# Fewer ready-made transposed tiles: 31 instead of 40, none of them made during the attention heads

## The reference, cut to what matters

```
h = rms(x) ; P = h @ w_in -> q,k,v (3 x 1024 columns) and B,C,xc (3 x 1024 columns)
attn = 8 heads of differential attention (two softmaxes a head, QK norm, ALiBi)
conv = B * causal_conv3(C * xc)
x = x + concat(attn, conv) @ w_out
h2 = rms(x)
PEER: q = h2 @ w_q ; top-16 of 128 keys twice per head -> 16 of 16384 experts, 8 heads
x = x + sum over chosen experts of  v[e] * gelu(u[e] . h2) * gate
```

## Time and profile before

| | us |
|---|---|
| runs of the kernel | 3073.46, 3074.99, 3070.95 (median 3073.46) |
| the profiled execution, its own time | 3075.95 |
| its span | 3074.1 |
| PE busy in the span | 2942.8 (96%) |
| DVE busy | 2327.9 (76%) |
| ACT busy | 1013.9 (33%) |
| POOL busy | 1505.5 (49%) |
| L1215, the 160 transposes of DVE | 100.2 |
| mean granted clock of TensorE | 0.987 of full |

### The profile page before, as it was taken

One profiled execution on the slowest core, in us unless ns is written; L12 is line 12 of the kernel. 1 busy time (PEld: TensorE's weight loads), 2 busy tenths in 40 slices (PEclk: granted clock), 3 DMA queues, 4 the chain that ended last, 5 costly groups with the idle time before them and its releaser, 6 DMA issues.

```text
span 3074.1 us, 40948 instructions
## 1 busy us (share of the span) xinstructions
PE 2942.8 (96%) x15249; PEld 2612.5 (85%) x15249; DVE 2327.9 (76%) x3102; ACT 1013.9 (33%) x1245; POOL 1505.5 (49%) x906
## 2 busy tenths in 40 slices
PE   8999989899988999999999999999999999998999
PEld 6888767678878999999999999999998877877777
DVE  5444656664468898888889887788766988988898
ACT  3112323341223333333333333233323333333333
POOL 1000222210006666555656665566766877886762
PEclk9999999999999999999999999999999999999999
DMA  7777676767458898989989898899999999999998
GB/s 262 261 235 222 204 212 186 219 237 273 150 183 290 293 339 301 319 297 326 317 296 342 298 320 299 297 334 318 322 354 368 413 414 410 415 415 415 416 415 338
DMA packets 321776, 947.12 MB, mean 308 GB/s; under 512 B 62484, under 2 KB 179232, under 8 KB 232288
## 3 DMA queue, kind: packets, MB, share of 16 engines
q1 hardware_dynamic: 177040, 475.04, 42.7%
q0 software_dynamic: 107008, 439.75, 40.5%
q10 hardware_dynamic: 37584, 30.43, 3.0%
HBM read 849.56 MB, written 95.55 MB: 307 GB/s over the span
## 4 chain that ended last, share of the span: by engine, by line
PE 63%; DVE 13%; DMA 12%; issue 6%; ACT 4%; POOL 0%; ACTq 0%; DVEq 0%; SPq 0%; POOLq 0%
PE ps L1695 19%; PE ps L1697 19%; PE ps L1696 19%; DMA v_raw<-in_peer_v 8%; PE ps L1945 4%; DMA seg_rows<-in_peer_u 3%; DVE v_lo L1608 2%; DVE u_row L1569 2%; ACT v_hi L1096 1%; DVE uT_lo L1553 1%; DVE seg_turned L1215 1%; DVE uT_lo L1558 1%; DVE wc_lo L1184 1%; ACT uT_hi L1056 1%; DVE x_one L1650 0%
## 5 line engine op out<-in xcount | busy, mean ns | idle before, releaser
L1695 PE MATMUL ps<-hT_hi,uT_hi 128*128 128x384 f32 x2048 | 703.2, 343 | 28.3 <-DVE uT_lo L1553 25.0
L1697 PE MATMUL ps<-h2T_lo,uT_hi 128*128 128x384 f32 x2048 | 688.2, 336 | 0.0
L1696 PE MATMUL ps<-hT_hi,uT_lo 128*128 128x384 f32 x2048 | 687.0, 335 | 0.0
L759 POOL DMA_INDIRECT gate_grid<-gates,grid_cells x256 | 542.2, 2118 | 120.2 <-issue 76.5
L1695 PE MATMUL ps<-v_hi,a_hi 128*128 128x512 f32 x1024 | 405.2, 396 | 35.0 <-DVE v_lo L1608 33.4
L1695 PEld LDWEIGHTS ps<-hT_hi,uT_hi 128*128 128x128 f32 x2048 | 386.3, 189 | 38.3 <-DVE uT_lo L1553 31.1
L1697 PE MATMUL ps<-v_lo,a_hi 128*128 128x512 f32 x1024 | 402.6, 393 | 0.0
L1696 PE MATMUL ps<-v_hi,a_lo 128*128 128x512 f32 x1024 | 402.6, 393 | 0.0
L1096 ACT ACTIVATE v_hi<-v_raw 128x2048 fp32r<-128x2048 f32 x128 | 245.7, 1919 | 462.2 <-PE ps L1697 345.4
L1696 PEld LDWEIGHTS ps<-hT_hi,uT_lo 128*128 128x128 f32 x2048 | 386.6, 189 | 1.9
L1697 PEld LDWEIGHTS ps<-h2T_lo,uT_hi 128*128 128x128 f32 x2048 | 385.8, 188 | 0.0
(11 more groups left out here) (206 smaller groups left out, 4860.1 us busy)
## 6 DMA issues: line engine op xcount, KB each, us to landing
v_raw<-in_peer_v SPq DMA_DIRECT2D x128, 1024.0 KB, 15.2
u_tile<-in_peer_u SPq DMA_DIRECT2D x88, 1024.0 KB, 7.2
seg_rows<-in_peer_u SPq DMA_DIRECT2D x40, 1024.0 KB, 6.7
u_tile<-uT_all SPq DMA_DIRECT2D x40, 1024.0 KB, 7.3
uT_all<-seg_turned SPq DMA_DIRECT2D x100, 256.0 KB, 6.4
w_raw<-in_w_in SPq DMA_DIRECT2D x24, 1024.0 KB, 6.3
wc_raw<-in_w_in SPq DMA_DIRECT2D x48, 512.0 KB, 7.4
gate_grid<-zeros POOLq DMA_DIRECT2D x16, 1024.0 KB
```

The costliest lines, as they stand in the source:

```text
L759: pool.indirect_dma_start(out=gate_grid, out_offset=bass.IndirectOffsetOnAxis(ap=grid_cells[:, d, col:col + 1], axis=0), in_=gates[:, 2 + ...
L1695: mm(out, a_hi, b_hi, start=first, stop=False)
L1696: mm(out, a_lo, b_hi, start=False, stop=False)
L1697: return mm(out, a_hi, b_lo, start=False, stop=last)
```

## The change

The heads make no ready-made tiles any more. Each of the five chunks in the loop of the projections makes four (the fourth after the split of the next chunk's quarter 1). The three at the end of the projections stay (now numbers 21, 22 and 23), and the seven in the output projection. All stores are issued by SP, none by POOL. The sweep finds 31 tiles ready (1, 3, ... 61) and lets PE transpose the other 97.

```diff
-TURNED = 40
-TURNED_QKV = 3 * (QKV_CHUNKS - 1)
-TURNED_HEADS = TURNED_QKV + 4 + 2 * (HEADS - 1)
-KEPT_BY_POOL = 1 + 2 * (HEADS - 1)
-KEPT_BY_SP = TURNED - KEPT_BY_POOL
+TURNED = 31
+TURNED_QKV = 4 * (QKV_CHUNKS - 1)
+TURNED_FIRST = TURNED_QKV + 4
...
 # SP, load_weights, behind load_quarter of every quarter
-                        if turned is not None and (q > 0 and turned == 0 if isinstance(c, int) else q != 1):
-                            keep_turned(3 * c + (turned + max(q - 1, 0)))
+                        if turned == 0 and not (isinstance(c, int) and q == 0):
+                            keep_turned(4 * c + (q - 1))
+                        elif turned is not None and turned > 0 and not isinstance(c, int) and q != 1:
+                            keep_turned(3 * c + (turned - 3 + max(q - 1, 0)))
...
 # SP, between the projections and the heads
             conv_piece(0, 0)
             conv_piece(0, 1)
-            for n in range(2):
-                keep_turned(TURNED_QKV + 1 + n)
+            for n in range(3):
+                keep_turned(TURNED_QKV + 1 + n, last=n == 2)
             with sp.Fori(0, CT - 1) as j:
                 for p in range(PIECES):
                     sp.wait_ge(wc_ready, PIECES * j + p + 1)
                     conv_piece(j + (p + 2) // PIECES, (p + 2) % PIECES)
-                    if p in (3, 5):
-                        next_rows(2 * j + (TURNED_QKV + 3 + p // 5))
...
 # POOL: the stores of number 18 and of two tiles a head are gone
-            keep_turned(TURNED_QKV + 3)
...
-                    keep_turned(TURNED_QKV + 4 + 2 * j)
...
-                    keep_turned(TURNED_QKV + 5 + 2 * j)
...
 # DVE, the loop of the projections
                 split_wi(c, 2)
-                turn_rows(3 * c + 1, "qkv")
+                turn_rows(4 * c + 1)
                 split_wi(c, 3)
-                turn_rows(3 * c + 2, "qkv")
+                turn_rows(4 * c + 2)
                 split_wi(c + 1, 0)
                 keep_qkv(c)
-                turn_rows(3 * c + 3, "qkv")
+                turn_rows(4 * c + 3)
                 split_wi(c + 1, 1)
+                turn_rows(4 * c + 4)
...
 # DVE, a head
                 combined(0)
-                if not last:
-                    turn_rows(2 * j + (TURNED_QKV + 4), "heads", range(2))
                 biased(2)
                 combined(1)
-                if not last:
-                    turn_rows(2 * j + (TURNED_QKV + 4), "heads", range(2, 4))
                 biased(3)
...
                 if not last:
-                    turn_rows(2 * j + (TURNED_QKV + 5), "heads")
                     norm_qk(j + 1, 1)
```

More of the change, by code:

```diff
@@ L408, in decoder_layer @@
         seg_stored = sem("seg_stored")
-        seg_kept = sem("seg_kept")
         u_tile_in = sems("u_tile_in", 2)
@@ L462, in load_rows @@
                 sp.dma_start(seg_rows[:, :], u_table[bass.ds((2 * n + 1) * P, P), :]).then_inc(seg_in, 16)
-            def next_rows(n):
-                sp.wait_ge(seg_ready, 4 * n + 4)
-                load_rows(n + 1)
             def keep_turned(n, last=False):
@@ L487, in load_weights @@
                     sp.wait_ge(w_used[0], QKV_CHUNKS + 1)
-                    load_rows(turned + 3)
+                    load_rows(turned)
                 with sp.Fori(1, chunks - 1) as c:
@@ L493, in load_weights @@
                     load_quarter(weights, chunks - 1, q + 2, order)
-                    if turned is not None and q == 0:
-                        keep_turned(turned + 3 * (chunks - 1), last=turned > 0)
+                    if turned == 0:
+                        keep_turned(4 * (chunks - 1) + q - 1)
+                    elif turned is not None and q == 0:
+                        keep_turned(3 * (chunks - 1) + turned - 3, last=True)
             for t in range(TB):
@@ L550, in _ @@
             load_mix(MIX_ORDER[3])
-            load_weights(OUT_CHUNKS, w_out_v, QKV_CHUNKS, MIX_ORDER, begun=3, turned=TURNED_HEADS - 3)
+            load_weights(OUT_CHUNKS, w_out_v, QKV_CHUNKS, MIX_ORDER, begun=3, turned=TURNED_FIRST)
             sp.wait_ge(w_ready, 4 * (QKV_CHUNKS + OUT_CHUNKS) - 1)
@@ L595, in _ @@
             sp.wait_ge(wq_ready, 4)
-            sp.wait_ge(seg_stored, 16 * QUADS * KEPT_BY_SP)
-            sp.wait_ge(seg_kept, 16 * QUADS * KEPT_BY_POOL)
+            sp.wait_ge(seg_stored, 16 * QUADS * TURNED)
             for i in range(PEER_HEADS - 2):
@@ L705, in zero_cells @@
                                zeros[:, :].unsqueeze(1).to_broadcast([P, 8, GRID])).then_inc(grid_done, 16)
-            def keep_turned(n):
-                pool.wait_ge(seg_ready, 4 * n + 4)
-                store_turned(pool, n, seg_kept)
-            keep_turned(TURNED_QKV + 3)
             pool.wait_ge(head_mean, 1)
@@ L718, in _ @@
                     store_o(j - 1)
-                if j < HEADS - 1:
-                    keep_turned(TURNED_QKV + 4 + 2 * j)
                 pool.wait_ge(head_mean, 2 * j + 2)
@@ L828, in split_weights @@
                 if isinstance(c, int) and (c, before) == (0, QKV_CHUNKS) and q < 2:
-                    act.wait_ge(seg_kept, 16 * QUADS * KEPT_BY_POOL)
+                    act.wait_ge(seg_stored, 16 * QUADS * TURNED_FIRST)
                     nc.scalar.activation((wo0_hi if q == 0 else w_hi[1])[:, :, :], wo_raw0, ACT.Copy).then_inc(w_hi_ready, 1)
@@ L996, in split_wq @@
                 nc.scalar.activation(part[:, :, :], raw[:, :, :], ACT.Copy).then_inc(wq_hi_ready, 1)
-            act.wait_ge(seg_stored, 16 * QUADS * KEPT_BY_SP)
+            act.wait_ge(seg_stored, 16 * QUADS * TURNED)
             split_wq(0, 0, early=True)
@@ L1201, in _, with turn_rows @@
             low(0, 3)
-            def turn_rows(n, stage, parts=range(4)):
-                if parts[0] == 0:
-                    dve.wait_ge(seg_in, 16 * n + 16)
-                    if isinstance(n, int) and n == 0:
-                        pass
-                    elif stage == "heads":
-                        dve.wait_ge(seg_kept, 16 * QUADS * (n - (TURNED_QKV + 3)))
-                    else:
-                        dve.wait_ge(seg_stored, 16 * QUADS * (n if stage == "qkv" else n - KEPT_BY_POOL))
-                for q in parts:
+            def turn_rows(n):
+                dve.wait_ge(seg_in, 16 * n + 16)
+                if not (isinstance(n, int) and n == 0):
+                    dve.wait_ge(seg_stored, 16 * QUADS * n)
+                for q in range(4):
                     v.transpose(seg_turned[:, :, 4 * q:4 * q + 4, :].rearrange("p r k e -> p k r e"),
@@ L1217, in turn_rows @@
                         .then_inc(seg_ready, 1)
-            turn_rows(0, "qkv")
+            turn_rows(0)
             dve.wait_ge(vec_in, 16 * 10)
@@ L1238, in _ @@
                 split_wi(c, 2)
-                turn_rows(3 * c + 1, "qkv")
+                turn_rows(4 * c + 1)
                 split_wi(c, 3)
-                turn_rows(3 * c + 2, "qkv")
+                turn_rows(4 * c + 2)
                 split_wi(c + 1, 0)
                 keep_qkv(c)
-                turn_rows(3 * c + 3, "qkv")
+                turn_rows(4 * c + 3)
                 split_wi(c + 1, 1)
+                turn_rows(4 * c + 4)
             split_wi(chunks - 1, 2)
-            turn_rows(TURNED_QKV + 1, "qkv")
+            turn_rows(TURNED_QKV + 1)
             split_wi(chunks - 1, 3)
-            turn_rows(TURNED_QKV + 2, "qkv")
+            turn_rows(TURNED_QKV + 2)
             dve.wait_ge(w_used[2], chunks)
@@ L1254, in _ @@
             keep_qkv(chunks - 1)
-            turn_rows(TURNED_QKV + 3, "qkv")
+            turn_rows(TURNED_QKV + 3)
             split_wc(0, 2)
@@ L1407, in rest_of_chunk @@
                 if not first:
-                    turn_rows(3 * c + (TURNED_HEADS - 1), "out")
+                    turn_rows(3 * c + (TURNED_FIRST - 1))
                 split_wo(c + 1, 0)
@@ L1411, in rest_of_chunk @@
                     add_mixed(c, t)
-                turn_rows(3 * c + TURNED_HEADS, "heads" if first else "out")
+                turn_rows(3 * c + TURNED_FIRST)
                 split_wo(c + 1, 1)
@@ L1417, in _ @@
                 split_wo(c, 2)
-                turn_rows(3 * c + (TURNED_HEADS - 2), "out")
+                turn_rows(3 * c + (TURNED_FIRST - 2))
                 rest_of_chunk(c)
```

## The result

| | before | after |
|---|---|---|
| median of the runs, us | 3073.28 (8 runs, 3066.62 to 3077.49) | 3080.18 (8 runs, 3076.98 to 3088.02) |
| the profiled execution, its own time | 3075.95 | 3080.20 |
| its span | 3074.1 | 3078.4 |

The changed kernel is slower by a quarter of a percent: ratio 1.0025, with a 95% interval of 1.0013 to 1.0036. By the ratio that is +7.7 us (0.0025 x 3073.28), by the two profiled executions +4.3. The forecast was 3094.6, +21. The sign was right, the size about three to five times too large.

The account below looks back on a forecast made before the run. DVE's waits for tile rows (48.5 us) were taken to stall PE in the heads; PE bounds the projections. 18.2 + 21.3 + 2 - 31 + 10.6 = +21.1 on 3075.95, less 2.5 to the median: 3094.6, range 3074 to 3107.

Parts of the forecast that it names:

- Projections, +18.2: Projections: with a fourth tile a chunk, tiles follow every 12.05 us against PE's 10.88 a quarter; PE ends 18.2 us later.
- rival 1: Projections: the tile chain keeps up, round 11.1 against 10.88; sum +3.1, 3076.6 us; chance 18%.
- rival 2: Projections: every tile, 23 too, finds its buffers free; head 0 starts +10.8, sum -7.6, 3065.9 us; chance 6%.
- rival 3: Projections: the tile chain gets slower, round 13.3 us; sum +41.8, 3115 us; chance 9%.
- Piece 2, +21.3: Between projections and heads: piece 2 of the convolution weights loads behind tile 23's transposes and stores; PE stands, +21.3 us.
- Half clock, +2: Start of head 0: PE comes out of 22 us of rest at half clock, ten long matmuls lose about 0.2 each; +2.
- sweep, +10.6: Sweep: nine tiles more need PE's transposes, head 4 9.1 us and tile 63 1.5; +10.6 us.
- Heads, -31: Heads: without tiles, six periods fall from 48.3 to 43.2 us, head 0 gives 0.3; -31, bounds -28 and -34.
- POOL's stores were off the path: Heads: claimed POOL's stores of the ready-made tiles were off the path; no gain was counted for removing them.
- At nothing: Output projection, its first weights' wait for stores, and loads from `u` in place of `uT_all`: no change, 0 us.
- Rival 4: Heads: waits for convolution weights replace the removed wait; heads save 12 in place of 31, 3113 us; chance 5%.

Follow-up runs that it names:

- run 10: Run 9's kernel without tile 23, so 30 ready-made tiles; 3061.07 us (one run).
- Run 8: Run 2's kernel plus four idle transposes a chunk in the projections, with the fourth tile's two waits but no loads or stores; 3043.13 us (one run).
- run 1: The changed kernel with piece 2 of head 0's convolution weights asked for before SP waits for tile 23's transposes; 3071.93 us, ratio 0.9987.
- run 4: The kernel before with a fourth tile in each of five chunks of the projections, heads as before, 45 tiles; 3099.08 us, ratio 1.0087.
- run 2: The kernel before without the heads' 14 ready-made tiles, nothing else changed, 26 tiles; 3046.27 us, ratio 0.9914.
- run 6: Run 2's kernel with the heads' 56 transposes put back on idle data, without loads, stores or waits; 3042.65 us (one run).
- run 3: The kernel before with one tile a head, at DVE's second place, in place of two, 33 tiles; 3041.43 us, ratio 0.9898.
- run 5: Run 3's kernel with POOL storing each tile in the next head, behind its clears and output store; 3037.69 us, ratio 0.9902.
- run 7: Run 2's kernel with 4 MB of idle loads and stores a head, no transposes, no DVE instruction waiting for them; 3050.38 us (one run).
- run 9: Run 1's kernel with splits of pieces 0 and 1 and piece 2's load ahead of tile 22, tile 23 stored later; 3061.57 us (one run).

## Why the prediction was right in sign and wrong in size

*Projections, +18.2: right, a little low.* Round 12.15 for 12.05. Head 0's first matmul less the pause before it says when PE ended the projections: 330.49 - 21.07 = 309.4, where it was 289.64 - 1.09 = 288.55, so +20.9 (run 10 has 20.3). Run 8 shows that the transfers' round carries it. Rivals 1 and 2, which let the chain keep up, are out, and so is rival 3 with 13.3 us. The Trainium skill, "DMA: Bandwidth & Descriptors", section "Anatomy of one DMA", had led to an estimate of 9.5 us for the round; the trace has 12.15, so the trace disagrees with what I worked out from it. That says little against the Trainium skill: its section is on a transfer that GpSimd issues, here SP issues them, and my estimate counted five transfers as one with nothing beside them.

*Piece 2, +21.3: right.* The pause grew by 21.07 - 1.09 = 20.0. The chain of steps (tile 22, its stores, tile 23, SP's stores, the piece, its split, the copies) was right event by event, each within 2 us. That the two terms together are so close, 39.5 for 40.9, is luck in part: one was 2.7 too low and the other 1.3 too high. What the chain did not say is that there are two brakes in a row, of 10 us each (runs 1 and 10). I did not read the place behind tile 22, of the splits on DVE and of the load on SP, as a brake of its own; the expectation of run 4 went wrong on just that.

*Half clock, +2, and sweep, +10.6: nearly right* (+2.3 and +9.4). Behind the pause the granted clock of the changed kernel from 330 to 336 us is 0.55 of full, about the lower of the two levels (1.2 of 2.4 GHz), and 1.00 from 336 on. Nine tiles cost 9.4, 1.04 each, just below the estimate of 1.1 to 1.8.

*Heads, -31: this step failed.* The mechanism was right (the wait for rows goes and PE becomes the bound), and the term was mis-sized: it measured -47.7. "A head without tiles takes 43.2" is the number: it is 40.9 (runs 2 and 6, and the changed kernel). I took it from head 0, as the middle between 43.7 (44.05 less 0.3) and 42.7 (less the 1.0 for ACT too), with its other pauses "that stay". But head 0 made two tiles as well, and it shared the queues with 4 MB of rows and stores. Nor did it have its rows "nearly in time": DVE stood 4.48 us for them, as its timeline before shows, and only PE's wait for that was short.

```profile
312.88 1.30 DVE L1215 STREAM_TRANSPOSE seg_turned<-seg_rows 128x512 f32<-128x512 f32 x2 [4.48 <-DMA seg_rows<-in_peer_u]
```

The pauses of 0.7 to 1 us were not a limit of the head. They were the late landing of weight pieces behind the tiles' stores: run 3 keeps them with one tile a head, run 5 loses them by moving the stores alone, run 7 has smaller ones from transfers without transposes. By 3 and 5 "POOL's stores were off the path" was wrong too: with one tile a head, its stores cost the 1 us.

In numbers, the six periods, 289.9 against 245.4, gave 44.5, and head 0, where I took 0.3 (its own 43.2 would have made it 0.85), gave 3.15 (44.05 - 40.90). The windows of head 0's period before and after show what it still had in it:

```profile
309.43:353.48 44.05, 41.83 (x204) 32.34 (x202) 29.99 (x66) 16.02 (x32) 11.68 (x14) 1.00 0.69 202
```
```profile
352.56:393.46 40.90, 40.90 (x204) 32.50 (x202) 25.37 (x58) 16.12 (x32) 7.30 (x6) 1.00 0.36 102
```

PE stood 2.2 us of it, the 1.02 for ACT and the 0.79 of the earlier trace rows among them, and its 204 matmuls took 0.9 longer at the same clock. Why they did is not shown.

Bounds of -28 and -34 were far too tight: both came from the same head as the value itself. The waits of the trace would have helped. PE waits 31.8 us in the heads of before for `probs` alone:

```profile
PE ps L1788 <- DVE probs L1329: 31.8, 15, 5.0
```

That is already more than the whole of my term, and the slower work of PE stands on top. In the seven periods PE's idle time is 32.3 and its longer work 15.4 (the windows above, mean clock 0.96 against 1.00).

*At nothing: nearly.* The stretch from the output projection to the sweep was 1.8 longer, the end 2.3 shorter. No experiment aims at either. Over the twelve traces of this study the first lies between 261.6 and 263.8 and the second between 750.7 and 756.6, so neither difference is a finding.

*Rival 4*, that the weights would hold the shorter heads, was wrong in direction: the pieces land sooner (4.8 us in the median for 7.4), and PE has no wait in the seven periods.

So the gain of the heads, 47.7, was almost enough. It went to the stages around it: 40.9 + 2.3 up to head 0, for the five more tiles of the projections and their places, and 9.4 for the nine fewer in the sweep.

**The version that beats both** is run 5: 3037.7, by its ratio of 0.9902 1% or 30 us below the kernel before. It makes one tile a head in place of two, at DVE's second place, and POOL stores it at the head of the next one. It has 33 tiles, with three a chunk. Run 3, which differs only in the place of the stores, is as far below by its ratio, 0.9898.

## What to carry to other kernels

A stage's floor is not its best instance while that instance still does some of the work that is to go. Work it out from the other side as well: the sum of the waits in the stage, and the slower clock behind them, is a first bound of what the stage can give back.

A chain of load, compute and store through one buffer has a round of its own. Compare it with the period of the stage beside it, and count the slots left free: with three slots in four 12 us fit beside 10.9, with four in four each round pushes everything behind it.

In a queue that takes its work in order, look at every load behind a wait, and at every step that frees a buffer for that load. Here a place behind tile 23 and one behind tile 22 cost 10 us each before head 0, and order alone gave both back for its start (run 9). Some 5 us of that came back as a wait within head 0, until tile 23 was left out (run 10).

## What the runs showed that I had not expected

- 1 MB of stores costs 1 us a head or nothing, depending on when it is issued (periods of about 42.0 and 40.9 in runs 3 and 5, median landing of the 512 KB pieces 7.0 and 4.6 us), with the DMA engines busy 0.60 and 0.59 of the time.
- Moving 238 GB/s in the heads (run 7) hurts less than waiting for 1 MB of rows: 0.6 us a head against some 6, the latter by difference.
- The stretch behind the sweep, with the DMA engines busy all the time (share 1.00 from 2340 to 3070 us, before and after), takes 750.7 to 756.6 us from one trace to another in kernels that do the same there. Differences of less than 6 us in single runs mean nothing here without the stages.
